# Gate tiles first, parity-ordered columns, and three turns moved from the matrix engine to GpSimd transfers

## The reference

```python
a, gate = jnp.split(h @ w_pw1 + b_pw1, 2, axis=-1)
u = a * jax.nn.sigmoid(gate)
dw = lax.conv_general_dilated(u, w_dw[:, None, :], window_strides=(1,),
    padding=((CONV_WIDTH - 1, 0),), feature_group_count=D_MODEL, ...) + b_dw   # 31 taps, causal, per channel
mu, var = mean(dw), mean((dw - mu)**2)                                          # over the 1024 channels
z = jax.nn.silu((dw - mu) * lax.rsqrt(var + EPS) * ln_g + ln_b)
return z @ w_pw2 + b_pw2
```

## Time and profile before

| what | value |
|---|---|
| median of three timed runs | 1105.5 us (1105.3 to 1105.76) |
| profiled execution, its own time | 1105.78 us |
| its span in the trace | 1104.0 us (1.78 us lie around it) |
| PE, DVE, ACT busy | 1099.4, 831.6, 615.5 us |
| granted TensorE clock | 1.00 throughout |

### The profile page before, as it was taken

The page is one execution under the profiler, slowest core; times in us unless marked ns, Lnnn a source line. Parts: engine busy times, 40 slices in busy tenths (PEclk is TensorE's granted clock), DMA queues, the critical chain, the costliest instruction groups (busy, mean ns, idle before and its releaser), DMA issues.

```text
span 1104.0 us, 18914 instructions
## 1 busy us (share of the span) xinstructions
PE 1099.4 (100%) x7382; PEld 990.4 (90%) x7382; DVE 831.6 (75%) x1281; ACT 615.5 (56%) x964; POOL 36.2 (3%) x53
## 2 busy tenths in 40 slices
PE   9999999999999999999999999999999999999998
PEld 9999888888888988889899998888888789888887
DVE  6977897775676887776669867777666879877753
ACT  6656555554545656555545455666444777656631
POOL 0030000000000000000010000000001110000000
PEclk9999999999999999999999999999999999999999
DMA  8544455555485555555645545555554325555551
GB/s 318 199 159 185 169 202 187 188 195 205 148 262 165 186 180 192 191 191 191 223 158 171 202 169 186 191 191 191 191 208 152 137 77 196 187 191 191 196 195 68
DMA packets 33209, 203.78 MB, mean 185 GB/s; under 512 B 3936, under 2 KB 7264, under 8 KB 9824
## 3 DMA queue, kind: packets, MB, share of 16 engines
q1 hardware_dynamic: 32160, 202.12, 52.3%
q10 hardware_dynamic: 960, 0.45, 0.2%
HBM read 200.33 MB, written 2.23 MB: 183 GB/s over the span
## 4 chain that ended last, share of the span: by engine, by line
PE 98%; DMA 1%; SPq 0%; ACT 0%; DVE 0%; issue 0%; POOL 0%; DVEq 0%; ACTq 0%
PE banks L440 46%; PE banks L453 24%; PE banks L416 6%; PE banks L419 6%; PE banks L422 6%; PE banks L493 3%; PE banks L476 1%; PE banks L482 1%; PE banks L479 1%; DMA raw_t<-w 1%; PE banks L1716 1%; PE banks L1702 0%; PE banks L528 0%; PE banks L863 0%; PE banks L506 0%; PE banks L871 0%
## 5 line engine op out<-in xcount | busy, mean ns | idle before, releaser
L347 DVE TENSOR_TENSOR lo_t<-raw_t,hi_t 128x1024 fp32r<-128x1024 f32 x364 | 439.3, 1218 | 12.9 <-ACT hi_t L341 11.7
L341 ACT ACTIVATE hi_t<-raw_t 128x1024 fp32r<-128x1024 f32 x364 | 376.2, 1050 | 105.3 <-PE banks L453 39.2
L440 PE MATMUL banks<-x,hi_t 128*128 128x512 f32 x1536 | 362.6, 391 | 0.0
L440 PEld LDWEIGHTS banks<-x,hi_t 128*128 128x128 f32 x1536 | 283.7, 188 | 56.3 <-issue 0.4
L453 PEld LDWEIGHTS banks<-x,lo_t 128*128 128x128 f32 x1536 | 193.5, 191 | 5.4
L453 PE MATMUL banks<-x,lo_t 128*128 128x256 f32 x1536 | 195.7, 283 | 0.0
L440 PE MATMUL banks<-f,hi_t 128*128 128x512 f32 x704 | 164.1, 390 | 0.0
L440 PEld LDWEIGHTS banks<-f,hi_t 128*128 128x128 f32 x704 | 130.6, 188 | 26.1
L597 DVE TENSOR_TENSOR scr<-banks,scr 128x512 f32<-128x512 f32 x88 | 60.4, 690 | 75.3 <-ACT scr L666 75.0
L453 PEld LDWEIGHTS banks<-f,lo_t 128*128 128x128 f32 x704 | 87.6, 192 | 1.9
L453 PE MATMUL banks<-f,lo_t 128*128 128x256 f32 x704 | 88.2, 283 | 0.0
(11 more groups left out here) (210 smaller groups left out, 1094.7 us busy)
## 6 DMA issues: line engine op xcount, KB each, us to landing
raw_t<-w SPq DMA_DIRECT2D x182, 1024.0 KB, 4.9
f<-shifts SPq DMA_DIRECT2D x16, 287.0 KB, 4.6
raw_t<-w SPq DMA_DIRECT2D x3, 512.0 KB, 9.7
h<-xT SPq DMA_DIRECT2D x4, 256.0 KB, 7.7
out<-h SPq DMA_DIRECT2D x8, 128.0 KB, 3.7
cst<-consts SPq DMA_DIRECT2D x1, 800.0 KB, 9.8
shifts<-scr SPq DMA_DIRECT2D x5, 144.0 KB, 3.7
raw_t<-w SPq DMA_DIRECT2D x2, 256.0 KB, 5.4
```

The lines of the kernel that those rows point to most:

```text
L341: e.activation(hi_t[:, p % RING, :], raw_of(p), ACT.Copy).then_inc(s_hi, 1)
L347: e.tensor_tensor(lo_t[:, p % RING, :], raw_of(p), hi_t[:, p % RING, :].bitcast(F32), ALU.subtract).then_inc(s_lo, 1)
L440: m = e.matmul(halves(banks[:, to[j], :]), hi_t[:, slot, r * P:(r + 1) * P], parts[:, ks[j], :, :], start=ks[j] == 0 and not low_first, st ...
```

## The change

First, "gate-first": the two last tile blocks of the first product's weights are exchanged, so that unit 7 makes its gate by `broad_run` and then its a by `tile`. The gate goes on to ACT and DVE while PE makes a, and a needs no copy and no `add`. Second, the columns of `dw` stay in parity order (all even tokens, then all odd): diagonals and turn matrix are laid out for it, `take` reads and writes plain rows, and only `dve_out` interleaves the tokens again. `dve_diagonals` writes its 1024 elements in two strided instructions. Third, units 0 to 2 are no longer turned on PE: there are four row buffers, and POOL issues four transfers per unit from the row buffer straight to `dw`, each of 64 partitions of 512 bytes, and `take` works in place. Last, unit 0 of the norm gets its high part by a Silu of its own, `pe_first_blocks` makes the eight blocks of n = 0 ordered by kind (eight high x high, eight low x high, eight high x low, which alone wait for `fl`), and `pe_keep_warm(7)` becomes 5. The core of the diff:

```diff
         diags = [scratch(C3 + n * PIECE, PIECE) for n in range(NE)]
-        assert C3 + NE * PIECE <= SCR and NS * 8 * SW <= (KF - KD) * 2 * T
-
-        crows = [sq[:, n, :] for n in range(2)]
+        assert C3 + NE * PIECE + T <= SCR and NS * 8 * SW <= (KF - KD) * 2 * T
+
+        crows = [sq[:, 0, :], sq[:, 1, :], ssum[:, :], scratch(C3 + NE * PIECE, T)]
+        N_MOVED = 3
+        s_moved = [sem(f"moved{n}") for n in range(N_MOVED)]
...
-                broad_run(e, G_PW1 + 16 * u, [CPAIRS[u % 3]] * KD + [CPAIRS[u % 3] + 1] * KD, [*range(KD), *range(KD)], x2, KD - 1,
-                          (lambda k: x_of(2, k)) if u == 0 else None, LAST_LATE if u == 0 else range(2 * KD))
+                if u < KD - 1:
+                    broad_run(e, G_PW1 + 16 * u, [CPAIRS[u % 3]] * KD + [CPAIRS[u % 3] + 1] * KD, [*range(KD), *range(KD)], x2,
+                              KD - 1, (lambda k: x_of(2, k)) if u == 0 else None, LAST_LATE if u == 0 else range(2 * KD))
+                else:
+                    broad_run(e, G_PW1 + 16 * u, [CPAIRS[u % 3] + 1] * KD, range(KD), x2, KD - 1)
+                    for k in range(KD):
+                        tile(e, G_PW1 + 16 * u + KD + k, banks[:, CPAIRS[u % 3], 0:T], k, x2, k == 0, k == KD - 1)
...
-                if u == 5:
-                    pe_turn(e, 0)
-                    pe_turn(e, 1)
...
                 pe_conv(e, u)
-                pe_turn(e, u - 1)
+                if u - 1 >= N_MOVED:
+                    pe_turn(e, u - 1)
...
-            pe_keep_warm(e, 7)
-            pe_out_blocks(e, 2, G_PW2, N_CONF, range(KD), 0, 8 * N_CONF)
+            pe_keep_warm(e, 5)
+            pe_first_blocks(e)
+            pe_out_blocks(e, 2, G_PW2, N_CONF, range(KD), 8, 8 * N_CONF)
             pe_out_rest(e, 2, G_PW2, N_CONF, range(KD))
+
+        def pe_first_blocks(e):
+            def product(j, weights, half, start):
+                dst = banks[:, OUT_BANKS[j // 2], (j % 2) * T:(j % 2 + 1) * T]
+                slot, r = piece(e, G_PW2 + j)
+                return e.matmul(dst, weights[:, slot, r * P:(r + 1) * P], f2[:, 0, half, :], start=start, stop=False,
+                                skip_group_check=True)
+
+            high, low = f_of(2, 0)
+            e.wait_ge(s_hi, G_PW2 // 8 + 1)
+            e.wait_ge(*high)
+            for j in range(KD):
+                product(j, hi_t, 0, j % 2 == 0)
+            e.wait_ge(s_lo, G_PW2 // 8 + 1)
+            for j in range(KD):
+                product(j, lo_t, 0, False)
+            e.wait_ge(*low)
+            for j in range(KD):
+                m = product(j, hi_t, 1, False)
+            m.then_inc(s_tiles, 1)
...
-            if u >= 6:
+            if 4 <= u < 4 + N_MOVED:
+                e.wait_ge(s_crow, u - 3)
+            if u == KD - 1:
                 e.wait_ge(s_dw, u - 3)
...
-                if u >= 2:
-                    e.wait_ge(s_turned_c, u - 1)
-                e.activation(crows[u % 2], banks[:, CONV_BANKS[u], 0:T], ACT.Copy).then_inc(s_crow, 1)
+                if u >= 4:
+                    e.wait_ge(s_moved[u - 4], 64)
+                e.activation(crows[u % 4], banks[:, CONV_BANKS[u], 0:T], ACT.Copy).then_inc(s_crow, 1)
...
+                if j == 0:
+                    e.activation(fh[:, 0, :], dw[:, 0, :], ACT.Silu, scale=colv("ln_g", 0),
+                                 bias=colv("ln_b", 0)).then_inc(s_fh, 1)
                 e.activation(dsq[:, j % NQ, :], dw[:, j, :], ACT.Silu, scale=colv("ln_g", j),
                              bias=colv("ln_b", j)).then_inc(s_cz, 1)
-                e.wait_ge(s_cz, j + 1)
-                e.activation(fh[:, j, :], dsq[:, j % NQ, :], ACT.Copy).then_inc(s_fh, 1)
+                if j:
+                    e.wait_ge(s_cz, j + 1)
+                    e.activation(fh[:, j, :], dsq[:, j % NQ, :], ACT.Copy).then_inc(s_fh, 1)
...
-            e.tensor_tensor(diags[u % NE].rearrange("p (a c) -> p a c", c=16), stretch(cv[:, V_MASK:V_MASK + 16], 1, 64),
-                            stretch(by_tap, 2, 16), ALU.mult).then_inc(s_diag, 1)
+            for o in range(2):
+                m = e.tensor_tensor(diags[u % NE].rearrange("p (a c o) -> p a c o", c=16, o=2)[:, :, :, o],
+                                    stretch(cv[:, V_MASK:V_MASK + 16], 1, 32), stretch(by_tap[:, o:64:2], 2, 16), ALU.mult)
+            m.then_inc(s_diag, 1)
...
+                gate = dv.mark(e.tensor_tensor(ct_r[u % 2][:, T:2 * T], banks[:, CPAIRS[u % 3] + 1, 0:T], cb[:, 0:T], ALU.add))
+                e.wait_ge(dv.sem, gate)
...
-                n = dv.mark(e.tensor_tensor(both[:, 0, :], both[:, 0, :], rbc[:, :], ALU.mult))
-                e.wait_ge(dv.sem, n)
+                e.wait_ge(s_tiles, upto(G_PW1 + 16 * KD - 1))
+                e.tensor_tensor(both[:, 0, :], banks[:, CPAIRS[u % 3], 0:T], rbc[:, :], ALU.mult).then_inc(s_cup, 1)
+                e.wait_ge(s_cup, KD)
...
-                ps = banks[:, CONV_BANKS[u], 0:T].rearrange("p (o j) -> p j o", o=2)
-                to = dw[:, u, :].rearrange("p (j o) -> p j o", o=2)
-                e.wait_ge(s_turned_c, u + 1)
+                to = dw[:, u, :]
+                if u < N_MOVED:
+                    e.wait_ge(s_moved[u], 64)
+                    turned = to
+                else:
+                    e.wait_ge(s_turned_c, u - N_MOVED + 1)
+                    turned = banks[:, CONV_BANKS[u], 0:T]
                 if u < 2:
-                    e.tensor_scalar(to, ps, colv("b_dw", u), None, ALU.add).then_inc(s_dw, 1)
+                    e.tensor_scalar(to, turned, colv("b_dw", u), None, ALU.add).then_inc(s_dw, 1)
                 else:
-                    by = shift.rearrange("p (j o) -> p j o", o=2)
-                    e.scalar_tensor_tensor(to, ps, colv("b_dw", u), by, ALU.add, ALU.subtract).then_inc(s_dw, 1)
+                    e.scalar_tensor_tensor(to, turned, colv("b_dw", u), shift, ALU.add, ALU.subtract).then_inc(s_dw, 1)
...
+            for u in range(N_MOVED):
+                e.wait_ge(s_crow, u + 1)
+                for o in range(2):
+                    for r in range(2):
+                        e.dma_start(dw[64 * r:64 * r + 64, u, o * P:(o + 1) * P],
+                                    crows[u][o:P:2, r * P:(r + 1) * P]).then_inc(s_moved[u], 16)
...
+    pw1 = mixed(tiles(pw1[:, 0:1024]), tiles(pw1[:, 1024:2048]))
+    pw1 = _np.concatenate([pw1[:, 0:14], pw1[:, 15:16], pw1[:, 14:15]], axis=1)
+    parts += [flat(pw1), outer(a["conv_w_pw2"][0], range(8), N_CONF)]
```

More of the change, by code:

```diff
@@ L736, in dve_out @@
                     for j in (2 * pair, 2 * pair + 1):
-                        e.scalar_tensor_tensor(h[:, j, :], ps[:, (j % 2) * T:(j % 2 + 1) * T], colv(bias, j), h[:, j, :],
-                                               ALU.add, ALU.add).then_inc(s_h, 1)
+                        by_token = h[:, j, :].rearrange("p (j o) -> p j o", o=2)
+                        e.scalar_tensor_tensor(by_token, ps[:, (j % 2) * T:(j % 2 + 1) * T].rearrange("p (o j) -> p j o", o=2),
+                                               colv(bias, j), by_token, ALU.add, ALU.add).then_inc(s_h, 1)
                 if pair:
@@ L1284, in pe_turn @@
                     turn = cv[:, V_TURN + 64 * odd:V_TURN + 64 * odd + 64]
-                    m = plain(e, banks[64 * r:64 * r + 64, CONV_BANKS[u], odd * P:(odd + 1) * P], turn, crows[u % 2][:, r * P:(r + 1) * P])
+                    m = plain(e, banks[64 * r:64 * r + 64, CONV_BANKS[u], odd * P:(odd + 1) * P], turn, crows[u % 4][:, r * P:(r + 1) * P])
             m.then_inc(s_turned_c, 1)
@@ L1306, in act_conformer @@
                 hi_to(e, c)
-                e.wait_ge(s_tiles, upto(c - 1))
+                if u < KD - 1:
+                    e.wait_ge(s_tiles, upto(c - 1))
+                else:
+                    e.wait_ge(s_tiles, upto(c - KD - 1))
                 if u:
                     e.wait_ge(s_cup, u)
-                e.activation(halves(cb), c_pair(u, 1), ACT.Copy).then_inc(s_cside, 1)
+                if u < KD - 1:
+                    e.activation(halves(cb), c_pair(u, 1), ACT.Copy).then_inc(s_cside, 1)
+                else:
+                    e.activation(cb[:, 0:T], banks[:, CPAIRS[u % 3] + 1, T:2 * T], ACT.Copy).then_inc(s_cside, 1)
                 if u < KD - 1:
@@ L1340, in act_conformer @@
             e.wait_ge(s_conv_half, 1)
-            e.wait_ge(s_turned_c, last - 1)
-            e.activation(crows[last % 2][:, 0:P], banks[:, CONV_BANKS[last], 0:P], ACT.Copy).then_inc(s_crow, 1)
+            e.wait_ge(s_turned_c, last - 4 - N_MOVED + 1)
+            e.activation(crows[last % 4][:, 0:P], banks[:, CONV_BANKS[last], 0:P], ACT.Copy).then_inc(s_crow, 1)
             e.wait_ge(s_conv, KD)
-            e.activation(crows[last % 2][:, P:T], banks[:, LAST_HALF, P:T], ACT.Copy).then_inc(s_crow, 1)
+            e.activation(crows[last % 4][:, P:T], banks[:, LAST_HALF, P:T], ACT.Copy).then_inc(s_crow, 1)
             squares(7, 1)
@@ L1370, in add @@
```

(17 more changed lines are left out.)

1 line of the change is left out of this document (added).

## The result

The changed kernel takes 1111.87 us (median of 6 executions, 1108.95 to 1113.76) against 1105.63 before (6 executions), a ratio of 1.0052 [1.0042, 1.0063]: slower by some 6 us. I had forecast 1108.2. Two things catch the eye before any detail: the executions spread over 4.8 us where those of the kernel before spread over 1.1, and the profiled one, 1108.95 us with a span of 1107.1, is the fastest of the six. So the trace of after shows a mild case, 3.2 us above the profiled execution of before.

What follows compares the result with a forecast made beforehand. PE was taken to bound the kernel. Turns saved 1.27 and 0.60 us, gate-first cost 0.10, waits for transfers 3.4 and 1.1: +2.7 us, so 1108.2 us by the median, range 1103.6 to 1110.8.

Steps and rivals of the forecast that it cites:

- What bounds the kernel, and where the change turns: PE sets the end; the change turns on PE's wait for the takes behind unit 6, reached at 324.4.
- Turns taken from PE: Turns of units 0 and 1 between units 5 and 6 save 1.27 us, unit 2's behind unit 7 saves 0.60.
- gate-first: Eight tiles of unit 7 by `tile` in place of `broad_run` cost PE 0.10 us; no gain counted.
- parity order: Strided halves of DVE's diagonals cost at most 1.22 us more each, counted as 0.
- The eight transfers: Units 0 and 1: issues of 0.97 us each and a 2.5 us landing make PE wait 3.4 us behind unit 6.
- rival 1: The transfers are hidden, with no wait for `s_dw` behind unit 6: -1.8 us, 1103.7; chance 0.40.
- rival 4: The new transfers land like the big ones, in 3.8 us: +5.3 us, 1110.8; chance 0.08.
- Unit 2: Its four transfers land at T + 6.4 against a needed `take(2)` start of T + 5.3: +1.1 us in the tail.
- T + 6.4: Forecast landing of unit 2's four transfers, T being the end of unit 2's row copy, 334.84 before.
- rival 3: PE's clock falls from 2.4 to 1.2 GHz in the wait behind unit 6: +3 us, 1111; chance 0.07.
- Norm and second product: PE starts the second product 0.67 us ahead, stood off again before j = 0, n = 7; counted as 0.
- The sum: -1.27 - 0.60 + 0.10 + 3.4 + 1.1 = +2.7 us; chance of this forecast with both waits 0.38.

Runs made afterwards that it cites:

- early_two: Changed kernel with ACT's row copies of units 0 and 1 made earlier and unit 2's turn back on PE: 1105.16 us, 0.9995 of the kernel before.
- two_moves: Changed kernel with the turn of unit 2 back on PE, units 0 and 1 still by transfers: 1111.53 us, ratio 1.0047 to the kernel before.
- fill: Changed kernel with 12 unused small matmuls before PE's wait for the takes of units 0 and 1: 1108.18 us, ratio 1.0019 to the kernel before.
- act_queue: Changed kernel with the eight transfers of units 0 and 1 issued by ACT instead of POOL: 1111.66 us, ratio 1.0049 to the kernel before.
- early_copies: Changed kernel with ACT's row copies of units 0 and 1 ahead of the weight piece that waits: 1105.81 us, ratio 0.9994 to the kernel before.
- first_only: Kernel before with only the extra Silu, reordered first blocks and 5 small matmuls instead of 7: 1106.03 us, ratio 0.9999 to the kernel before.

## Why the prediction was wrong

Two terms of the sum failed, and the time needed both: the landing of the eight transfers, put at 2.5 us, and the lowered clock behind the wait, put at nothing.

- **What bounds the kernel, and where the change turns: right.** PE sets the end; it reached the sum at 324.4 as forecast and waited there for the second `take`.
- **Turns taken from PE, gate-first, parity order: right.** Units 5 and 6 take 324.44 - 313.16 = 11.28 us in early_two, the forecast value to the hundredth, and without the transfers the rest measures 0.9997. Two diagonals took 2.49 us in place of 2.36, hidden.
- **The eight transfers: a wait where I had put it, but the landing was the first step that failed.** I took 2.5 us, below the medians of the earlier trace rows, because 32 KB stay on the chip. It is 4.9 to 6.5 by the median of the eight, and what counts is the last of them: 7.5 us at most in after, 8.7 in two_moves. With 97% of the transfer engines in use a small transfer landed no sooner than a big one. The issue was off the other way: I took 0.97 from the slowest of SP's, and it is 0.58. That the wait came out at all is partly luck: by an estimate with 0.58 and my 2.5 the last would have landed at 324.2 and PE would have waited 0.2 us, which is close to rival 1. From first issue to last landing I had 8 x 0.97 + 2.5 = 10.3 us; it was 11.6 in after and 12.8 in two_moves. I had also said that the time of ACT's row copies doesn't move; it lies between 314.0 and 316.9 from trace to trace. PE's wait is 2.2 us with the copies at 314.07 (after) and 6.1 at 316.86 (two_moves), where I had 3.4. In fill, with copies at 316.25, filling and wait together are some 4.9. My upper bound of 3.8 us for the landing (rival 4) was a median and so no bound; the earlier trace rows had 7.5 as the longest.
- The Trainium skill's fixed cost of about 2.0 us for each transfer (DMA: Bandwidth & Descriptors, Anatomy of one DMA), which I had beside my value, is approached only by unit 2's transfers where the engines are used to some 30% (medians of 1.9 us in after, 2.5 in fill, 2.7 in act_queue; 3.9 in early_copies, where they are used to 85% at first); the measurement decides. The estimate beside mine used the Trainium skill's 1 us to the first byte (DMA: Bandwidth & Descriptors, Specifications) as the time of an issue, which it is not: POOL's issues follow one another at 0.58 us. It gave a wait close to mine for the same reason as mine, one term too long and one too short.
- **Unit 2: about right.** In early_copies, where nothing before it is disturbed, DVE's `take` starts at T + 6.6 (332.73 to 339.30; forecast T + 6.4) and PE waits 1.19 us (forecast 1.1). In after it is T + 5.6 (337.50 to 343.09), in a stretch where the transfer engines were used to 31% at first, and PE's wait 0.64 us, about the turn that it saves.
- **The clock: the second step that failed.** I gave rival 3 a chance of 0.07 because no row showed a falling clock, and the sum has nothing for it. The clock fell in every execution of the changed kernel (mean 0.997 or 0.998) and cost 1.8 us after a wait of 2.2, 2.6 after one of 4.4 (act_queue) and 2.3 after one of 6.1. Kept near 1.00 by useless matmuls, the time fell to 1108.2. My price of 3 us for it was near; the chance was wrong. The rule of the Trainium skill that I named there (TensorE: Matmul & The Clock Gate, What's actually happening) holds here in its direction: the fence of stretches shows 0.50 behind the idle stretch, and 1.00 again with PE at work.
- **Norm and second product: right.** The 0.67 us were stood off before j = 0, n = 7, by 0.70 in first_only and in after, and stayed once the chain was shorter.
- **The sum.** For the heavy case it should have been -1.27 - 0.60 + 0.10 + 6.1 + 2.3 + 0.6 = +7.2 us; the median is +6.2, between this and the mild profiled case of +3.2. Against my +2.7, the wait has +2.7 more and the clock +2.3. With either of them alone the forecast would have become 1110.9 or 1110.5, at the end of the range, which was 1110.8 because it joined no long landing with the clock.

## What to carry to other kernels

A wait on several transfers lasts until the last of them has landed. With the transfer engines busy that was near the longest landing of much bigger transfers here (6.6 to 8.7 us for 32 KB, 7.5 for 287 KB), so measure from the first issue to the last landing, and cover that much. Look at more than one trace for the time at which the first issue can come; here it moved by 2.8 us. Where the matrix engine is the bound, price a wait together with the lowered clock behind it: here waits of 2.1 to 6.1 us, and one of 1.7 us behind three shorter ones, were followed by it, and single waits of 0.6 to 1.2 us were not. A consumer moved one unit on, or a producer taken out from behind an unrelated wait, was worth 5 to 6 us here, where the work saved was worth 1.9.

## What the runs showed of the hardware

Transfers of 32 KB within the chip's memory took 1.7 to 8.7 us from issue to landing. POOL's issue took 0.58 us each, and ACT's 0.71 (5.67 for eight), though its store of 144 KB has 0.37. Behind a wait of 2.17 us on PE its clock went to 1.2 GHz for some 3.3 us, from 0.4 us after the work had begun again; in the wait of 6.1 us it was at that level before the work began (0.50 from 329.2 on). The price does not grow in step with the wait: 1.8 us behind this one, 2.6 behind 4.4 us and 2.3 behind 6.1 us.
